# Moving 360 of 506 low-part subtractions of the weights from VectorE to GpSimd, in a two-block transformer kernel

## The reference

```python
for layer in range(DEPTH):
    h = rms_norm(x, norm_w[layer])
    proj = jnp.einsum('bsd,de->bse', h, w_in[layer])
    ...
    y_a = mamba2_branch(a_xbc, a_z, a_dt, ...)
    y_b = sliding_window_branch(b_q, b_k, b_v, b_z, ...)
    y_c = forgetting_attention_branch(c_q, c_k, c_v, c_f, c_z, ...)
    branch = jnp.einsum('bsiw,iwd->bsid', jnp.stack([y_a, y_b, y_c], axis=2), w_proj[layer])
    merged = jnp.sum(jax.nn.sigmoid(gates + gate_bias[layer]) * branch, axis=2)
    x = x + jnp.einsum('bsd,de->bse', merged, w_out[layer])
```

## Time and profile before

| | us |
|---|---|
| median of 3 runs (2186.74 to 2192.32) | 2190.89 |
| the profiled execution | 2192.32 |
| its span, first to last instruction | 2190.5 |
| PE busy | 2085.2 (95%) |
| DVE busy | 1377.5 (63%) |
| ACT busy | 1112.2 (51%) |
| POOL busy | 85.0 (4%) |

### The profile page before, as it was taken

The page is one execution under the profiler, slowest core; times in us unless marked ns, Lnnn a source line. Parts: engine busy times, 40 slices in busy tenths (PEclk is TensorE's granted clock), DMA queues, the critical chain, the costliest instruction groups (busy, mean ns, idle before and its releaser), DMA issues.

```text
span 2190.5 us, 36684 instructions
## 1 busy us (share of the span) xinstructions
PE 2085.2 (95%) x14870; PEld 1856.0 (85%) x14870; DVE 1377.5 (63%) x2394; ACT 1112.2 (51%) x1892; POOL 85.0 (4%) x64
## 2 busy tenths in 40 slices
PE   6999998998999998999999999999999979999997
PEld 6999987998999988998667786778888868998997
DVE  6687667565687666564365345655555556667776
ACT  5575465544585475564376233433333346645553
POOL 0311000000311000000000000000000000000000
PEclk9999999999999999999999999999999989999998
DMA  6645443665645443655122434333333333354551
GB/s 227 208 145 201 160 141 116 192 213 213 228 164 178 170 133 127 201 180 196 68 87 78 153 136 172 114 118 132 118 126 113 128 116 106 126 185 144 184 189 52
DMA packets 93321, 330.65 MB, mean 151 GB/s; under 512 B 10080, under 2 KB 13408, under 8 KB 92896
## 3 DMA queue, kind: packets, MB, share of 16 engines
q1 hardware_dynamic: 93152, 328.30, 44.2%
HBM read 327.08 MB, written 1.18 MB: 150 GB/s over the span
## 4 chain that ended last, share of the span: by engine, by line
PE 81%; DVE 9%; ACT 7%; issue 1%; DMA 1%; POOL 0%; SPq 0%; DVEq 0%; ACTq 0%
PE ps L878 22%; PE ps L880 22%; PE ps L879 22%; DVE t_lo L1554 3%; ACT t_hi L1239 2%; PE ps L932 2%; PE ps L891 2%; PE ps L892 2%; PE ps L893 2%; PE ps L1150 1%; DMA t_raw<-in_W 1%; PE ps L1160 1%; PE ps L1171 1%; PE ps L1022 1%; DVE t_B L1663 1%
## 5 line engine op out<-in xcount | busy, mean ns | idle before, releaser
L878 PE MATMUL ps<-t_RB,t_hi 128*128 128x256 f32 (+1 forms) x3712 | 1169.1, 315 | 8.4 <-DVE t_RB L1842 3.5
L879 PE MATMUL ps<-t_RB,t_hi 128*128 128x256 f32 (+1 forms) x3712 | 1147.7, 309 | 0.0
L880 PE MATMUL ps<-t_RB,t_lo 128*128 128x256 f32 (+1 forms) x3712 | 1147.3, 309 | 0.0
L1554 DVE TENSOR_TENSOR t_lo<-t_raw,t_hi 128x1024 fp32r<-128x1024 f32 (+1 forms) x506 | 616.8, 1223 | 493.9 <-ACT t_hi L1239 488.0
L878 PEld LDWEIGHTS ps<-t_RB,t_hi 128*128 128x128 f32 x3712 | 711.0, 192 | 80.5 <-issue 28.0
L1239 ACT ACTIVATE t_hi<-t_raw 128x1024 fp32r<-128x1024 f32 (+1 forms) x506 | 525.0, 1042 | 441.1 <-PE ps L880 403.5
L879 PEld LDWEIGHTS ps<-t_RB,t_hi 128*128 128x128 f32 x3712 | 711.6, 192 | 34.8 <-issue 1.9
L880 PEld LDWEIGHTS ps<-t_RB,t_lo 128*128 128x128 f32 x3712 | 710.8, 191 | 35.5
L1980 DVE SCALAR_TENSOR_TENSOR t_A<-ps,t_V,t_A 128x510 f32<-128x510 f32 (+1 forms) x176 | 102.2, 612 | 94.1 <-ACT t_A L1514 92.6
L1514 ACT ACTIVATE t_A<-ps,t_V 128x512 f32<-128x512 f32 (+1 forms) x88 | 48.5, 577 | 127.8 <-PE ps L880 127.8
L1953 DVE SCALAR_TENSOR_TENSOR t_X<-ps,t_MOD,t_X 128x256 f32<-128x256 f32 x168 | 72.2, 477 | 43.8 <-PE ps L880 43.8
(11 more groups left out here) (294 smaller groups left out, 1952.2 us busy)
## 6 DMA issues: line engine op xcount, KB each, us to landing
t_raw<-in_W SPq DMA_DIRECT2D x586, 512.0 KB, 3.4
t_A<-cu_scratch SPq DMA_DIRECT2D x8, 512.0 KB, 5.5
t_B<-cu_scratch SPq DMA_DIRECT2D x8, 512.0 KB, 4.7
t_raw<-in_W SPq DMA_DIRECT2D x16, 256.0 KB, 2.9
t_A<-in_C SPq DMA_DIRECT2D x2, 1536.0 KB, 8.1
t_X<-in_X SPq DMA_DIRECT2D x2, 512.0 KB, 4.3
t_X<-in_X SPq DMA_DIRECT2D x1, 1024.0 KB, 7.7
out<-t_X SPq DMA_DIRECT2D x1, 1024.0 KB, 4.8
```

The costliest lines, as they stand in the source:

```text
L878: mm(o, hi[:, w], xh(k), start=k == 0 and j == 0, stop=False)
L879: mm(o, hi[:, w], xl(k), start=False, stop=False)
L880: i = mm(o, lo[:, w], xh(k), start=False, stop=k == nkt - 1 and m == u.x[1] - 1)
L1554: tt(t.lo[s][:, 0:w], t.raw[r][:, 0:w], t.hi[s][:, 0:w].bitcast(F), ALU.subtract).then_inc(*up("dve", ("split", u.i)))
```

## The change

`plan()` gives each split its engine. Before it was always `"dve"`; now it is DVE only for some, and POOL for the others:

```diff
             fn, h, w = o.chunks[u.i]
-            u.x = (w, len(rows), "dve")
+            u.x = (w, len(rows), "dve" if u.i >= NS and u.i % (4 if u.x[0] else 2) == 1 else "pool")
             rows.append((fn, h, w))
```

## The result

The changed kernel takes 2204.49 us (median of 4 runs, 2203.31 to 2207.19), the kernel before 2189.93 on the same chip (2186.74 to 2192.32): ratio 1.0066, 95% interval 1.0052 to 1.0081. It is slower by 14.6 us; 16 us less were forecast. The profiled execution is 2203.31 us, its span 2201.0.

A forecast was written before the change was run, and what follows sets the result against it. PE was taken as the bound, busy 2085.2 of 2190.5 us, with gains only in its pauses. Terms -7.0 - 2.0 - 8.0 - 1.0 + 1.0 + 1.0 = -16.0 us against 2192.3 gave 2176.3, stated as 2176 (2165 to 2184).

The forecast's parts named there:

- What shares a port: Step on DVE and POOL taking turns: POOL's subtraction holds two-SBUF-operand DVE instructions up to 2.4 us, is held up to 1.2.
- terms 3 and 4: First and second pauses of PE in each sliding-window stage: -8.0 and -1.0 us for both layers.
- DVE's busy time: Sign that the forecast holds: DVE busy for near 950 to 1000 us over the whole kernel.
- Start, -7.0: Kernel start, splits 0 to 4 moved: `norm1` steps shorten, last low part at about 19 instead of 26.1 us; -7.0 (-7.5, -5).
- Second layer's `norm1`, -2.0: Second layer's `norm1`, split 136 moved: one step loses its wait and subtraction; -2.0 us (-2.5, -1).
- First pauses, -8.0: First PE pause of each sliding-window stage, near 311 and 800 us: `exp` may start earlier; -8.0 us (-10, 0).
- Second pauses, -1.0: Second PE pause of each sliding-window stage: ACT's copies end late anyway, little goes; -1.0 us for both layers (-6, +3).
- `fox_prep`, +1.0: The eight `fox_prep` on POOL: subtractions queued behind them, such as split 20, come close to late; +1.0 us (0, +8).
- SP's queue and the SSM, +1.0: SP's loads asked for 1.2 us later, +1.0 (0, +3); second layer's SSM pause 0 (-2.6, +3).
- the steady stages cost nothing: Stages without PE pauses: POOL needs 7.1 of 11.4 us per four halves, keeps up, so moved subtractions cost 0 there.
- nothing arrives: Rival: the start's gain is returned at the next point where ACT or a DMA is last; 2187 to 2192 us, chance 0.08.
- The port one: Rival: in sliding-window attention POOL's port turns eat the gain, terms 3 and 4 fall to +1; 2186 us, chance 0.15.

The follow-up runs named there:

- By halves: Changed kernel with each of the 360 POOL subtractions issued as two instructions on half the columns; 2190.72 us, ratio 1.0003 to the kernel before.
- by quarters: Changed kernel with each of the 360 POOL subtractions issued as four instructions on a quarter of the columns; 2195.29 us, ratio 1.0022 to the kernel before.
- e8: Changed kernel with only 31 subtractions on POOL: 0 to 4, 136, 138 and most ahead of each sliding-window stage's first pause; 2171.53 us, ratio 0.9918 to before.
- e14: As e8, but with all 20 subtractions of each sliding-window stage on POOL, 47 in all; 2171.38 us.
- e11: Changed kernel with only the start's 5 subtractions and 46 beside the SSM chunks on POOL; 2185.10 us, ratio 0.9979 to the kernel before.
- e4: Changed kernel with 143 subtractions on POOL, only in steady stages, all others including the start on DVE; 2194.22 us, ratio 1.0014 to the kernel before.
- the fill: Kernel before, all subtractions on DVE, plus 355 useless POOL memsets of a scratch tile at the moved ones' events after the start; 2185.49 us.

## Why the prediction was wrong

**The failed step is the one headed "What shares a port".** I had read from the earlier trace rows that a POOL subtraction can hold a DVE instruction by up to 2.4 us, and then applied this only to `probs`. DVE has 1,888 instructions besides its subtractions of weights, most of them short, and many read two SBUF tiles. Their sum rose from 1377.5 - 616.8 = 760.7 to 1224.0 - 209.9 = 1014.1 us, by 253 us or 0.7 us for each subtraction on POOL. By halves the rise is 181 us, by quarters 121. Outside terms 3 and 4 no term of the sum held it, and where such an instruction stands at the end of a chain that PE waits for, it is lost time and a slow clock behind it. The prediction's own sign of this was DVE's busy time, 950 to 1000 us forecast and 1224.0 measured.

By its terms:

1. Start, -7.0: right in mechanism and a little small; -8.4 alone, -8.7 in the shift of half 2, beyond the bound of -7.5.
2. Second layer's `norm1`, -2.0: right or a little large. PE's pauses there hold 5.6 us in e8 and 4.9 in the changed kernel instead of 6.3; from half 132 to 140 the shift moves by -1.9 and -0.9.
3. First pauses, -8.0: right in mechanism and too small. The shifts are -6.0 and -6.3, beyond the bound of -10.
4. Second pauses, -1.0: within its bounds. In the first layer 2.9 us come back there (halves 81 to 90). Terms 3 and 4 together are -9.4 against a forecast of -9.0. That the sum fits is luck: one is too small and the other has the wrong sign. e8 has -9.9, with term 2 in it. That ACT's copies would be last in this pause anyway is what e14 shows.
5. `fox_prep`, +1.0 (0 to 8): the stages cost 8.0. About 4 of it is the queue, as worked out in the prediction for split 20 and then called close; the rest is the port, in front of a `pv` of the first layer.
6. SP's queue and the SSM, +1.0: the SSM stages cost 3.6 (bounds +3 for each of the two). In e11 PE's wait for ACT's line 1368 in the second layer is 4.1 us instead of 2.6, as in the changed kernel. That SP had a part in it no run shows.

Missing: the scalar chain (+6.1), the late stages (+8.8) and what e4 costs (+4.3), 19.2 us in all. With terms 5 and 6 mis-sized by 9.6, that is 28.8 us, against 30.6 between a forecast change of -16.0 and a measured one of +14.6. The first two and term 5's half are shown to be the port; for e4 it is not shown. The sentence that the steady stages cost nothing holds as far as the profile of e4 goes, since no lateness arises in them there.

Of the rivals, "nothing arrives" had its place too: in e14 ACT is what is left of the second pauses. The port one had the mechanism and the wrong place: it looked for it where the gain was, in the sliding-window stage, where it took little, and not where DVE has a short chain that ends in a PE wait. "POOL's queue in the fox stages" set its threshold at 2.5 us for splits 14 and 20; POOL's large subtractions had a mean of 2.51, and in the first layer PE waited there. This rival was right in kind, for about 4 us of the 40 it gave. The rule of the Trainium skill ("Perfetto Trace Analysis", Optimizing Scalar/DVE Operations), that moving work between DVE and GpSimd might not help, was the better guide for 329 of the 360; for the other 31 it was not.

## What to carry to other kernels

Before moving work to GpSimd, list for each stage the VectorE instructions on PE's path that read two SBUF tiles, and the short TENSOR_SCALARs, and charge each up to a whole GpSimd instruction. Move only what stands in VectorE's queue ahead of a wait of PE, and leave the rest where it is: 31 moves gave 18.7 us, 329 more took 33 back. If much must go to GpSimd, try it in two pieces: here they gave 14 us back, and four pieces only 9, as GpSimd was then busy for 1192.2 us and late more often.

## What the runs showed of the hardware

- A DVE instruction of one SBUF input pays too, if it is the short TENSOR_SCALAR: line 1693, 128 x 8, takes 172 ns before, 1269 in the changed kernel and 246 beside the fill. The Trainium skill ("SBUF — State Buffer", Who interferes with whom) counts this operation among those that can take both of DVE's ports, where its operands meet certain conditions. The prediction had not counted it.
- Its record can overlap DVE's next one: at 620 us, beside a fill, the next instruction started 0.07 us after it and kept its usual 1.23 us. In the changed kernel all eight long ones of its 16 (2.3 to 2.4 us) end within 0.04 us of the end of a POOL subtraction.
- A POOL subtraction costs more in pieces: a mean of 2508 ns whole, 2 x 1.40 us in halves, 4 x 0.82 in quarters.
- The clock after a pause is a part of the price. The 4.7 us of waiting at 48 us moved PE by 7.1 us: 11 matmuls ran in the 2.15 us up to 50 us, where 18 fit at full pace, and 32 instead of 43 or 44 in the 5 us behind, at a granted clock of 0.67.
- How much the clock gives back after the same pause varies. From 300 to 400 us the kernel before and the one with the filling ghost have the same pauses (4.0 and 8.5 us); their windows are, before:

```profile
300.00:400.00 100.00, 87.52 (x717) 82.75 (x716) 65.08 (x113) 59.26 (x113) 0.00 (x0) 0.91 0.42 138
```

and beside the fill:

```profile
300.00:400.00 100.00, 87.53 (x732) 82.92 (x731) 66.60 (x109) 60.33 (x114) 17.14 (x18) 0.95 0.44 143
```

15 matmuls more at 119 ns are some 2 us. This may be a part of why that version is faster than before; what in it favours the clock stays open. The same holds for e4's 1.6 us above. Of parts of 2 to 4 us in the table, some may be of this kind.
